# One change to the scan steps of a two-block kernel: when ScalarE reads outputs, how keys are turned, where divisors and gates are made

## The reference

```python
r, k, v = xr @ w_r, xk @ w_k, xv @ w_v
w = -jax.nn.softplus(-(w0 + jnp.tanh(xw @ w1) @ w2)) - 0.5
a = jax.nn.sigmoid(a0 + (xa @ a1) @ a2)
g = jax.nn.sigmoid(xg @ g1) @ g2
...
# per head: S_t = S_{t-1} diag(decay) + (S_{t-1} a_t) b_t^T + v_t k_t^T ; y_t = S_t r_t
y = wkv7_scan(r_h, decay, k_h, v_h, -kk, kk * a_h)
mean = jnp.mean(y, -1, keepdims=True)
var = jnp.mean(jnp.square(y - mean), -1, keepdims=True)
y = ((y - mean) * lax.rsqrt(var + GN_EPS)).reshape(B, S, D)
y = y * ln_w + ln_b
bonus = jnp.sum(r_h * k_h * r_k, -1, keepdims=True) * v_h
return ((y + bonus.reshape(B, S, D)) * g) @ w_o
```

## Time and profile before

| | us |
|---|---|
| median of three runs (lowest, highest) | 2749.97 (2746.17, 2752.63) |
| the profiled run | 2751.65 |
| its span in the profile | 2749.6 |
| PE busy (share) | 2662.2 (97%) |
| DVE / ACT / POOL busy | 1491.8 / 1048.5 / 774.9 |
| first z copy of the scan to the last (L2026) | 763.86 to 889.74 |
| first product of `rwkv_o` (L312) | 909.80 |

### The profile page before, as it was taken

How to read it: one execution, slowest core, us unless ns; L and a number is a source line. 1 busy time by engine, 2 the same in 40 slices (tenths; PEclk the granted TensorE clock), 3 DMA queues, 4 the chain that set the end, 5 groups by cost and what they waited for, 6 DMA issues and landing times. The chain is left out here.

```text
span 2749.6 us, 41479 instructions
## 1 busy us (share of the span) xinstructions
PE 2662.2 (97%) x15710; PEld 2103.5 (77%) x15710; DVE 1491.8 (54%) x1925; ACT 1048.5 (38%) x1873; POOL 774.9 (28%) x707
## 2 busy tenths in 40 slices
PE   8999999899998999999999999999999999999999
PEld 6788888656787788888777766888888656888887
DVE  4477673474645776754477665544433366644332
ACT  6333332424455343333355545322222357322221
POOL 3231111351762411113003655311111064311100
PEclk9999999999999999999999999999999999999999
DMA  4223323311200232333221130323333200233333
GB/s 156 77 92 99 94 89 100 105 59 54 62 11 23 63 98 92 98 90 94 86 85 62 30 83 24 102 93 99 96 88 101 90 24 1 85 99 93 96 90 103
DMA packets 80554, 219.21 MB, mean 80 GB/s; under 512 B 21917, under 2 KB 22045, under 8 KB 80158
## 3 DMA queue, kind: packets, MB, share of 16 engines
q1 hardware_dynamic: 79262, 215.17, 25.7%
q10 hardware_dynamic: 1152, 2.10, 0.2%
HBM read 215.14 MB, written 2.10 MB: 79 GB/s over the span
## 5 line engine op out<-in xcount | busy, mean ns | idle before, releaser
L312 PE MATMUL psum<-rounded,high_r 128*128 128x512 f32 x3040 | 1201.0, 395 | 28.4 <-DVE rounded L400 9.9
L314 PE MATMUL psum<-rounded,high_r 128*128 128x512 f32 x3040 | 1188.0, 391 | 0.0
L316 PE MATMUL psum<-rounded,ring_low 128*128 128x512 f32 x3040 | 1187.7, 391 | 0.0
L337 ACT ACTIVATE high_r<-ring 128x1024 fp32r<-128x1024 f32 (+2 forms) x432 | 420.3, 973 | 1375.7 <-PE psum L316 1352.9
L342 DVE TENSOR_TENSOR ring_low<-ring,high_r 128x1024 fp32r<-128x1024 f32 (+2 forms) x432 | 525.7, 1217 | 538.8 <-ACT high_r L337 537.0
L312 PEld LDWEIGHTS psum<-rounded,high_r 128*128 128x128 f32 x3040 | 573.5, 189 | 181.5 <-issue 36.3
L316 PEld LDWEIGHTS psum<-rounded,ring_low 128*128 128x128 f32 x3040 | 573.5, 189 | 121.0
L314 PEld LDWEIGHTS psum<-rounded,high_r 128*128 128x128 f32 x3040 | 574.0, 189 | 117.7 <-issue 1.6
L786 DVE TENSOR_TENSOR arena<-psum,inverse 128x512 f32<-128x512 f32 x176 | 121.5, 691 | 314.3 <-PE psum L316 314.2
L639 POOL CAST rounded<-rows 128x512 f32 (+1 forms) x88 | 53.9, 613 | 785.4 <-DVE rows L791 785.4
L435 POOL TENSOR_TENSOR arena<-resid 128x512 f32<-128x512 f32 x41 | 52.4, 1277 | 238.0 <-DVE resid L423 238.0
(11 more groups left out here) (419 smaller groups left out, 2731.3 us busy)
## 6 DMA issues: line engine op xcount, KB each, us to landing
ring<-in_up SPq DMA_DIRECT2D x176, 512.0 KB, 3.6
ring<-in_down SPq DMA_DIRECT2D x64, 384.0 KB, 3.1
ring<-in_down SPq DMA_DIRECT2D x64, 320.0 KB, 2.9
ring<-in_even_in SPq DMA_DIRECT2D x36, 512.0 KB, 3.4
ring<-in_sgu_in SPq DMA_DIRECT2D x16, 512.0 KB, 3.6
ring<-in_even_out SPq DMA_DIRECT2D x16, 384.0 KB, 3.1
ring<-in_qkv SPq DMA_DIRECT2D x12, 512.0 KB, 3.4
ring<-in_sgu_out SPq DMA_DIRECT2D x8, 512.0 KB, 3.6
```

Of the source, the lines that this page charges most:

```text
L312: nc.tensor.matmul(psum[:, m, :], high_r[:, r % HIGHS, blk], x_high, start=(k0 + k == 0), stop=False)
L314: nc.tensor.matmul(psum[:, m, :], high_r[:, r % HIGHS, blk], x_low, start=False, stop=False)
L316: mm = nc.tensor.matmul(psum[:, m, :], ring_low[:, r % R, blk], x_high, start=False, stop=end)
L337: nc.scalar.activation(high_r[:, r % HIGHS, 0:nk * P], ring[:, r % R, 0:nk * P], ACT.Copy).then_inc(unit_high, 1)
```

## The change

On ACT a step now copies keys, spreads blocks, copies the carried part, and reads the outputs of the step just ended last (`keep_y(k-1)` where it was `keep_y(k-2)` ahead of the carried copy). On PE `corrections_in` and `output` are cut in parts: the values' share of the next corrections comes between the two halves of the outputs, the state's share of the outputs goes behind `carry` and ahead of `change_corrected`. Keys are turned by sixteen 64x64 products with an identity into banks 6 and 7 instead of four transposes into bank 6. The divisors are made on ACT alone, as a logarithm (with scale and constant) and an exponential; DVE normalises only n=0, in steps 10 and 11, and POOL does n=1 to 3 in two more operations each. The four gates of step 16 are spread: one in step 15, two in step 16, the last with `gate_rest(0)` behind the last output. Two `occupy` calls use bank 3 for bank 7.

```diff
@@ -1188
+def states_of(u):
+    return [x for x in range(2) if x in entered(u + x)]
@@ -1473,7 +1477,7 @@
...
             if u == 0:
-                occupy(7, 5)
+                occupy(3, 5)
             pe.wait_ge(masked, 3 * u + 1 if u else 3)
...
@@ -1485,7 +1489,7 @@
...
-        def corrections_in(k):
+        def values_in_corrections(k):
...
@@ -1503,9 +1507,12 @@
...
                     mm.then_inc(z_half_valued, 1)
-            if entered(k):
-                pe.wait_ge(s_kept, k)
-                pe.wait_ge(z_half_valued, k + 1)
+            if not entered(k):
+                mm.then_inc(z_done, 1)
+        def state_in_corrections(k):
+            pe.wait_ge(s_kept, k)
+            pe.wait_ge(z_half_valued, k + 1)
             for i in range(2):
...
@@ -1538,7 +1545,7 @@
...
         def turn_keys(u):
-            _, cs, i0 = place(u)
+            i0 = place(u)[2]
             if u:
...
@@ -1547,15 +1554,18 @@
...
                 for i in range(2):
-                    tr = nc.tensor.transpose(psum[:, 6, (2 * w + i) * P:(2 * w + i + 1) * P],
-                                             arena[:, slot + i0 + i, cs], con("ident"))
-            tr.then_inc(bk_turned, 1)
+                    for e in range(2):
+                        for x in range(2):
+                            at = (2 * w + i) * HD
+                            mm = nc.tensor.matmul(psum[half(x), 6 + e, at:at + HD], arena[half(e), slot + i0 + i, tokens(u, x)],
+                                                  con("ident")[half(e), half(e)], start=True, stop=True)
+            mm.then_inc(bk_turned, 1)
...
         def key(u, x, w, i, e):
-            at = (2 * w + i) * P + e * HD
+            at = (4 * e + 2 * w + i) * HD
             return keys(u)[half(x), at:at + HD]
...
@@ -1639,33 +1649,39 @@
...
-        def output(u):
-            _, _, i0 = place(u)
-            pe.wait_ge(round_kept, u + 2)
+        def state_in_output(u):
+            i0 = place(u)[2]
             if u:
...
                 turn_bonus(BONUS_TURNED.index(u))
-            has_state = [x for x in range(2) if x in entered(u + x)]
             for i in range(2):
                 for e in range(2):
-                    for x in has_state:
+                    for x in states_of(u):
                         mm = nc.tensor.matmul(psum[half(x), 2 + e, i * HD:(i + 1) * HD], arena[half(e), RR + i0 + i, tokens(u, x)],
-                                         state(u + x - 1)[half(e), 1 - x, i, :], start=(i == 0), stop=False)
+                                              state(u + x - 1)[half(e), 1 - x, i, :], start=(i == 0), stop=False)
             mm.then_inc(y_entered, 1)
-            for n in range(2):
-                if n:
-                    pe.wait_ge(y_entered, u + 1)
-                for i in range(2):
-                    for x in range(2):
-                        e = n if x == 0 else 1 - n
-                        o = psum[half(x), 2 + e, i * HD:(i + 1) * HD]
-                        nc.tensor.matmul(o, kept(u)[half(x), e, 1, i, :], corrected(u + x)[half(x), e, i, :],
-                                         start=(i == 0 and x not in has_state), stop=False)
-                    for x in range(2):
-                        e = n if x == 0 else 1 - n
-                        o = psum[half(x), 2 + e, i * HD:(i + 1) * HD]
-                        mm = nc.tensor.matmul(o, kept(u)[half(x), e, 2, i, :], values(u, i, e, x), start=False, stop=(i == 1))
+        def output(u, n):
+            if n == 0:
+                pe.wait_ge(round_kept, u + 2)
+            else:
+                pe.wait_ge(y_entered, u + 1)
+            for i in range(2):
+                for x in range(2):
+                    e = n if x == 0 else 1 - n
+                    o = psum[half(x), 2 + e, i * HD:(i + 1) * HD]
+                    nc.tensor.matmul(o, kept(u)[half(x), e, 1, i, :], corrected(u + x)[half(x), e, i, :],
+                                     start=(i == 0 and x not in states_of(u)), stop=False)
+                for x in range(2):
+                    e = n if x == 0 else 1 - n
+                    o = psum[half(x), 2 + e, i * HD:(i + 1) * HD]
+                    mm = nc.tensor.matmul(o, kept(u)[half(x), e, 2, i, :], values(u, i, e, x), start=False, stop=(i == 1))
+            if n == 0:
+                return
             if u in BONUS_SUMMED:
...
@@ -1673,31 +1689,39 @@
...
         carry(0)
+        values_in_corrections(0)
         for k in range(STEPS):
             more = k + 1 < UNITS
-            corrections_in(k)
+            if entered(k):
+                state_in_corrections(k)
             if more:
                 turn_keys(k + 1)
-            if more and k:
-                score(k + 1)
-            if k == UNITS:
-                for n in range(4):
-                    gate(n)
+                if k:
+                    score(k + 1)
+            else:
+                gate(k - UNITS + 1)
             if k == 0:
-                occupy(7, 2)
+                occupy(3, 2)
             solve_blocks(k)
...
                 change_known(k)
+            if k == UNITS:
+                gate(2)
             round_of(k)
...
                 carry(k + 1)
-            if k == UNITS:
-                gate_rest(0)
+            if k:
+                state_in_output(k - 1)
             if left(k):
                 change_corrected(k)
-            if 0 < k < UNITS:
-                output(k - 1)
-        output(UNITS - 1)
+            if k:
+                output(k - 1, 0)
+            if k < UNITS:
+                values_in_corrections(k + 1)
+            if k:
+                output(k - 1, 1)
+        gate(3)
+        gate_rest(0)
         for i in range(3):
...
@@ -1834,7 +1858,7 @@
...
                 act.wait_ge(s_done, u - 1)
-            nc.scalar.activation(keys(u), psum[:, 6, :], ACT.Copy).then_inc(bk_kept, 1)
+            nc.scalar.activation(keys(u).rearrange("p (e f) -> p e f", e=2), psum[:, 6:8, 0:256], ACT.Copy).then_inc(bk_kept, 1)
...
@@ -1866,10 +1890,12 @@
...
-        def root(n):
-            act.wait_ge(var_ready, n + 1)
+        def root(n, kept_units):
+            act.wait_ge(y_kept, kept_units)
             x = by_heads(var, n)
-            nc.scalar.activation(x, x, ACT.Sqrt).then_inc(y_rooted, 1)
+            nc.scalar.activation(x, x, ACT.Ln, bias=con("eps", 1, 2), scale=1.0 / HD).then_inc(y_rooted, 1)
+            act.wait_ge(y_rooted, n + 1)
+            nc.scalar.activation(x, x, ACT.Exp, scale=-0.5).then_inc(y_inverted, 1)
...
@@ -1884,12 +1910,11 @@
...
                 spread(k + 1)
-            if k >= 2:
-                keep_y(k - 2)
-            if k + 1 < UNITS:
                 keep_carried(k + 1)
-            if k in (10, 12, 14, 16):
-                root((k - 10) // 2)
+            if k in (9, 11, 13, 15):
+                root((k - 9) // 2, k - 1)
+            if 0 < k < UNITS:
+                keep_y(k - 1)
             if k == 13:
...
@@ -1899,7 +1924,7 @@
...
         output_high(0)
-        root(4)
+        root(4, UNITS)
         for i in range(1, 4):
...
@@ -2048,28 +2073,15 @@
...
-        def normalise(n, of=slice(0, 32)):
-            dve.wait_ge(y_inverted, n + 1)
-            at = [(c, h) for c in (range(NCH) if n == 0 else (n - 1,)) for h in (range(8) if n == 0 else range(8, NH))]
-            for c, h in at[of]:
+        def normalise(of):
+            dve.wait_ge(y_inverted, 1)
+            for c, h in itertools.product(of, range(8)):
                 x = yt[:, c, h * HD:(h + 1) * HD]
...
-        def variance(n, kept_units):
-            dve.wait_ge(y_kept, kept_units)
-            x = by_heads(var, n)
-            nc.vector.tensor_scalar(x, x, 1.0 / HD, 64e-5, ALU.mult, ALU.add).then_inc(var_ready, 1)
-        def invert(n):
-            dve.wait_ge(y_rooted, n + 1)
-            x = by_heads(var, n)
-            nc.vector.reciprocal(x, x).then_inc(y_inverted, 1)
-            if n == 4:
-                dve.wait_ge(y_inverted, 5)
...
@@ -2094,7 +2106,6 @@
...
             if k == UNITS:
-                invert(3)
                 split_low(dve, Stream("rwkv_o"), 0, 0)
...
@@ -2105,19 +2116,11 @@
...
                 turn_back(1).then_inc(turned_back, 1)
-            if k in (9, 11, 13, 15):
-                variance((k - 9) // 2, k - 1)
-            if k in (10, 12, 14):
-                invert((k - 10) // 2)
-            if k in (11, 12):
-                normalise(0, slice(16 * (k - 11), 16 * (k - 10)))
-            if k in (13, 15):
-                normalise((k - 11) // 2)
-        normalise(3)
+            if k in (10, 11):
+                normalise(range(2 * k - 20, 2 * k - 18))
         for i in range(3):
             gate_output(i)
-        variance(4, UNITS)
-        invert(4)
+        dve.wait_ge(y_inverted, 5)
         for n, (with_, op) in enumerate(((spread_over(mean, 4), ALU.add), (spread_over(var, 4), ALU.mult),
...
@@ -2174,14 +2177,20 @@
...
             y, v = y_of(n), v_of(n)
```

(11 more changed lines are left out.)

8 lines of the change are left out of this document (4 added, 4 removed).

## The result

The changed kernel takes 2761.98 us (median of ten runs, 2758.18 to 2766.35), the kernel before 2752.36 beside it: a ratio of 1.0032, 95% interval 1.0023 to 1.0042. 2752.0 had been predicted, with 2743 to 2761 as its range; the time lies above it, and the sign, slower, is clear of the noise. The rise is 9.6 us, where 2.0 had been forecast. The profiled run took 2766.04 us, with a span of 2764.1.

A forecast was written before the change was run, and what follows sets the result against it. A scan step was taken as paced by a loop through ScalarE's key copy and output read, 7.4 us. Terms -2.0 + 1.0 + 1.5 - 1.9 + 1.1 + 4.9 - 5.5 + 2.9 gave +2.0: median 2752.0 us, range 2743 to 2761.

The forecast's parts named there:

- Part 2: Keys in 64x64 tiles: 28 more records a step, as many weight loads, risking instruction-supply pauses; +1.0 us, bounds 0 and 5.
- rival D: Instruction supply: the 64x64 keys meet a pause in nearly every step, 5 us instead of 1; 2756 us, chance 0.06.
- Part 1: Outputs read last, products reordered: the wait moves to the keys' copy, a step takes 7.3 for 7.43; steps 0 to 9 -2.0 us.
- the 6.4 of products alone: Time the matmul engine's products alone would need in a steady step, in us, against the 7.4 of the paced step.
- Part 3: Divisors by logarithm and exponential: two table loads per root, 3.0 us each, delaying output reads; +1.5 us in step 10.
- rival B: One table load serves all five roots, so each falls to 0.5 us; 2748 us, chance 0.12.
- step 10's term: Step 10: the root makes the output read 1.4 us late, with 0.2 for normalising on VectorE; +1.5 us.
- Part 4: Normalising moved mostly to GpSimd: steps 11 and 12 -1.9 us, 13 +1.1, 14 +4.9 (gate rows' spreading, clock fall), 15 -5.5.
- Part 5: Gates and tail, from step 16's z copy to the weight products: 22.9 us for 20.06, +2.9 rounded.
- Rival C: Longer stands make the clock fall repeatedly, 1.9 us each; with five falls beyond the sum's two, 2761 us; chance 0.20.
- the sign that I gave: Clock below 1 in three or more places would show the forecast wrong and the repeated clock falls right.

The follow-up runs named there:

- e1: The changed kernel with keys turned again by four 128x128 transposes into bank 6, all else as changed; ratio 1.0007 to the kernel before.
- e8: e6 with Sqrt roots, gates 2 and 3 before the last outputs, VectorE's low weight-tile part later, output read split, PE's output state products later; ratio 0.9975.
- e3: The changed kernel with divisors by one Sqrt on ScalarE and a reciprocal on VectorE; ratio 1.0024 to the kernel before.
- e6: e1 with the gate rows' spreading moved from behind step 13's output read to ahead of step 12's; ratio 0.9996 to the kernel before.
- e12: The changed kernel unaltered, run and profiled a second time; ratio 1.0042 to the kernel before.
- e11: The changed kernel with only the second load (512 KB, gate rows) issued two units later; 154.5 us from first z copy to first weight product, one run.
- e2: The kernel before with only the change's 64x64 keys; ratio 1.0036 to the kernel before.
- e4: The changed kernel with ScalarE's earlier order, outputs read one step late and ahead of the carried copy; ratio 1.0041 to the kernel before.

## Why the prediction was wrong, by its own steps

**Part 2, the keys: the step that failed.** It was taken as +1.0 with 0 and 5 as bounds, and rival D, a pause in nearly every step, had 0.06. Between e1 and the changed kernel, steps 0 to 9 differ by 7.5 us (68.9, 76.4), the stretch by 8.7, and the ratio by 0.25%, some 6.9 us: all above even the upper bound. The mechanism of rival D was the right one; its price was not. I had taken the pauses for single events (1.64 us) and multiplied their length by a count; they are what shows of PE running out of instructions. The profile before showed it too, had I asked: 96 instruction packets, in its scan every 4.0 us, with room of some 8% to the 3.7 of the changed kernel, against 28 records and 28 weight loads added to 490, and each of its six pauses ended 2.2 to 2.5 us behind a packet's start.

**Part 1, the steady step: right in mechanism, mis-sized by the supply.** The wait moved to L1582, behind the keys' copy; forecast 7.3, measured 7.13 where no pause falls (e1), 7.5 to 8.4 as changed. Steps 0 to 9 were forecast 71.9 without the keys' term; e1 has 68.9. Three more us were gained than I had thought, above all in steps 7 and 8, 6.15 and 6.92 in e1 for 7.39 and 9.09 before, where I had given 1.2 together. The fall of the clock at the earlier trace rows, which I had left in the sum, is gone there (1.00 in e1's steps 0 to 9). So the order pays in these steps, by 5.0 us, but only with wide keys. Over the stretch e1 is level with the kernel before all the same: its step 14 is 4.0 us longer and its tail 6.7. One number of the working had no row: the 6.4 of products alone. The parts listed there leave 6.9 without the stand; the step of 6.32 in e8 shows that 6.4 was near all the same.

**Part 3, roots: right on the loads, too dear in step 10.** Ten loads of 1.283 us, none shared: rival B fell, and with it the rule of the Trainium skill, "ScalarE: Activation LUTs", section "Table sets: the hidden batching unit", for the logarithm and the exponential. The delay of 1.4 us that I had put into step 10 did not come: 9.18 for 10.3, and 9.26 in e3 without the loads. Steps 11 to 12 were 16.69 for 16.8. In step 14 and the tail the loads did cost (e3: 2.6 and 2.1 us less). So step 10's term was 1.1 us too high, which hid that much of what the keys cost.

**Part 4: right.** Steps 13, 14 and 15 were 8.27, 11.72 and 5.38 for 7.8, 12.3 and 4.9. The stand and the fall of the clock in step 14 came (0.71), and e6 shows their cause: without the spread of the gate rows at that place the clock stays whole and the step is 3.4 us shorter. VectorE's normalising and scaling left step 15 as told.

**Part 5, the tail: mis-sized, 26.25 for 22.9.** To the last output it took 6.8 as forecast, in spite of a stand of 2.18: the sum of the round waited for VectorE's low part of a weight tile, itself behind ScalarE's high part. I had named 1 to 2 us at this place without adding them, and put them to GpSimd; ScalarE's high part was what VectorE waited for. Then:

```profile
896.94 1.67 PE L1628 MATMUL psum<-rows 128*128 128x512 f32 x2
898.54 2.09 PE L1635 MATMUL psum<-rows,work 32*128 32x512 f32 x8
...
905.14 1.11 PE L1649 MATMUL psum<-const,arena 128*128 128x128 f32 x4 [3.40 <-ACT psum L1889]
```

```profile
900.64 2.07 ACT L1902 ACTIVATE arena<-psum 128x512 f32<-128x512 f32 x4 [7.04 <-PE psum L1635]
...
908.77 2.38 DVE L2132 TENSOR_TENSOR arena<-arena,small 128x512 f32<-128x512 f32 x2 [1.73 <-ACT small L1898]
911.18 1.64 DVE L2132 TENSOR_TENSOR arena<-arena,work 128x512 f32<-128x512 f32 x1
912.86 0.69 DVE L2132 TENSOR_TENSOR arena<-arena 128x512 f32<-128x512 f32 x1
```

The four gate copies took 2.0, where my sum had the 0.6 of one: +1.4. Gate 3 ran at the lower clock (1.67 for 0.93): +0.7. VectorE's four operations took 4.8 for 4.0, the last turns and the start of the stream 2.9 for 2.5. These make the 3.3. The last two were to be had from the trace of before, where the same four operations (L2129) take 4.8 and the turns 2.9. (PE's timeline, then ACT's and DVE's, of the changed kernel.)

**Rival C**, repeated falls of the clock in the scan: not so. They were in steps 9 and 14 and the tail; before they had been in step 8 and the tail. By the letter of the sign that I gave, a clock below 1 in three or more places, C is met; the two falls beyond the sum by which it was to decide did not come. But the clock did take part elsewhere. The changed kernel's profile is 14.5 us longer, its stretch 7.9; the scan started 1.3 earlier, and what lies behind it, whose code is the same, took 1847.7 us for 1839.8, in e12 1847.8, in e11 1842.2, in e1 1837.1. A place with its windows, changed kernel first and then before:

```profile
1424.00:1428.00 4.00, 3.41 (x11) 2.21 (x12) 3.93 (x6) 1.81 (x3) 0.00 (x0) 0.81 0.29 113
1428.00:1432.00 4.00, 4.00 (x15) 3.15 (x15) 0.44 (x1) 0.00 (x0) 0.00 (x0) 0.77 0.00 0
...
1496.00:1500.00 4.00, 4.00 (x18) 3.64 (x17) 1.92 (x4) 2.27 (x7) 0.00 (x0) 0.50 0.00 0
```

```profile
1420.00:1424.00 4.00, 3.52 (x15) 2.31 (x16) 3.93 (x6) 1.82 (x3) 0.00 (x0) 1.00 0.29 110
1424.00:1428.00 4.00, 4.00 (x21) 3.35 (x20) 0.98 (x2) 0.59 (x1) 0.00 (x0) 1.00 0.00 0
...
1490.00:1494.00 4.00, 3.38 (x23) 3.06 (x24) 2.25 (x4) 2.65 (x10) 0.00 (x0) 1.00 0.00 0
```

Both have the same stand of 1.61 us for VectorE ahead of the first pair; all I can name that differs is that it comes 4.1 us later. How much the clock took can be read, though. Behind the stretch it was at its lower level for 20.5 us before, for 33.8 in the changed kernel and in e12, and for 7.5 in e1. At half the clock half of that is lost, by this estimate 10.3, 16.9, 16.9 and 3.8 us; less these, the parts took 1829.6, 1830.8, 1830.9 and 1833.3, and all fourteen traces lie between 1829.6 and 1833.9. So some 6.6 of the 7.9 us behind the stretch are the clock's. Why it falls in one kernel and not in the other stays open, and so does how far this enters the medians: they rose by 9.6, the stretch by 7.9 (e2: 9.0 and 4.0; e4: 10.6 and 3.2). The two profiled runs of the changed kernel have a mean clock of 0.988 and lie 4.1 and 2.7 us above their medians; its other runs have 0.989 to 0.992, the kernel before 0.990 to 0.996. For the pauses and the steps of the scan this leaves no doubt, since they are read within the stretch; of the whole kernel's 0.32%, a part may be the clock's.

## What to carry to other kernels

Where a loop is made of short products, count matmul and weight-load records per step and divide by what one instruction packet holds (here some 260): times the spacing of the packets (here 3.5 to 4.0 us on average) this estimates what the step takes, whatever the engines could do, and a change that makes one wide instruction into many small ones moves it. Look at the packets of the instruction queue before trusting a gain in a wait: e8 took a wait of 7.6 us away and got nothing for it. And of everything put between two waits, count each copy: four copies are four.

## What the runs showed of the hardware

Instruction packets of 16 KB came every 3.6 to 4.0 us on average in the scans with some 540 records a step (steps 1 to 8; 3.8 in e1 with 490, where PE hardly paused), never closer than 3.2, and PE took 71 records per us in the changed kernel (3952 in 55.7 us), 73 in e4 (2825 in 38.52). After 169 of 171 pauses PE resumed 1.8 to 2.9 us behind a packet's start. The loads of 768 and 512 KB, landed 5.9 to 7.4 us after the first was issued in the kernel before and the changed one, went with a gap of 5.2 to 6.7 us between packets in thirteen of fourteen traces; PE stood 2.8 us for it in the changed kernel and 0.8 in e1, where it had slack. The granted clock behind the scan fell at the same places in both profiles of the changed kernel (1426, 1495, 1584, 2147 and 2239 us in the first, each 1.1 to 1.2 later in the second) and at others in the kernel before (1318, 1704, 2332), for the same code.
